# One 512-column operand for the two parts of x in the recurrent passes

## The chip, the cores and the metric

The kernel runs on one core of one Trainium2 chip. Times are device microseconds (us) of that core. The comparison is between the median of several runs of the kernel before and of the kernel after; where the text works from a profile it says so, since that is one execution. The engines are TensorE (PE in the profile; PEld is its weight loading), VectorE (DVE), ScalarE (ACT), GpSimd (POOL) and SyncE (SP), which issues the DMAs.

## The reference, cut to what matters

Two model blocks follow each other, 256 tokens wide 2048 features, in float32. The change lies in the first block alone, in its recurrent branch:

```
xn = rms_norm(x, norm_pre_w)
z = xn @ w_in                       # u_lru: 2048 columns, g_lru: 2048 columns, then q, k, v, gates
u = centred_depthwise_conv(u_lru, conv_w, conv_b)          # 4 taps over the tokens
gate_r = sigmoid(block-wise u @ w_r + b_r); gate_i = sigmoid(block-wise u @ w_i + b_i)
log_a = -8 * gate_r * softplus(-lam);  a = exp(log_a)
b = sqrt(-expm1(2 * log_a)) * (gate_i * u)
h = scan(a, b) forwards + scan(a', b') backwards           # over the 256 tokens
y_a = h * silu(g_lru)
```

The rest of block one (keys and values, attention, merging, output) and two layers of block two come after it and are not touched.

## The kernel before

Every matrix product is made of three float32r products, since one alone is not exact enough: with x = x_hi + x_lo and w = w_hi + w_lo it sums w_hi·x_hi, w_hi·x_lo and w_lo·x_hi. ScalarE rounds each weight slot to w_hi (L273), VectorE subtracts to get w_lo (L281), and TensorE may use the slot when VectorE has counted it in the semaphore `split`. A slot holds 2048 weights per partition. Five slots form a ring; SyncE loads a slot when TensorE has finished with the slot five before it (`used`).

Slots 0 to 31 are the eight recurrent passes, four slots each. In pass i TensorE makes two tiles of u_lru (slots 4i and 4i+1, PSUM banks z0 and z1) and two of g_lru (slots 4i+2 and 4i+3, banks z2 and z3), each of 128 features by 256 tokens. A slot is 16 steps kk of three matmuls of 256 columns (`features`, L308). After them come sixteen matmul instructions for the gates of the recurrence (L1113), which read the convolved u. Slots 32 to 35 make the keys and 36 to 39 the values, with matmuls of 512 columns (`tokens`, L320); after slot 37 the keys are turned (L1146).

The other engines follow with a loop of their own, written out by hand. Its round i does the convolution of pass i and the gates and the scan of pass i-1. ScalarE: sigmoid of g_lru out of PSUM (`gate_inputs`, L560), eight sigmoids of the recurrence's gates (`gates`), rounding of slot 4i+3, four tanh, rounding of slot 4i+4, copy of u_lru out of PSUM (`input_copy`, L598), four exp, one sqrt (L590), rounding of slots 4i+5 and 4i+6, rounding of y (L602). VectorE: product of g_lru with its sigmoid (`open_gates`, L840), residual of slot 4i+3, residual of slot 4i+4, two convolutions (`convolve`, L829 and L833, four instructions each), the recurrence (L846, L850, four scans), residual of slot 4i+5, the output y (L860, L863), residual of slot 4i+6, the residual of y (L867). All engines run their queue strictly in the written order. In round 2 VectorE also prepares the angles of the rotary embedding (L889, L891 ahead of slot 13's residual; L356 to L363 between y and slot 14's residual), and before round 1 it has a chain of small steps for the softplus.

TensorE waits, before slot 4i+b (b = 0, 1), for `ucopied`, which frees bank zb; before slot 4i+2+b for `zcopied`, which frees bank z(2+b); and before the gates of pass i for `conv`, the eight steps of both convolutions.

Of the kernel before, what the change touches and what calls it, by code (L numbers as in the profile page):

```python
# [10 lines left out]
F32R = mybir.dt.float32r  # L11
I32 = mybir.dt.int32
ACT = mybir.ActivationFunctionType
ALU = mybir.AluOpType
AX_X = mybir.AxisListType.X

P = 128
D = 2048
T = 256
KT = D // P  # L20
# [12 lines left out]
LRU_PASSES = KT // 2  # L33
# [214 lines left out]
class Ring:  # L248
# [50 lines left out]
    def features(self, pe, n, out, x_hi, x_lo, each=None, whole=True):  # L299
# [9 lines left out]
        ins.then_inc(self.s.used, 1)  # L309

    def tokens(self, pe, n, quarter, outs, x_hi, x_lo):

        w_hi, w_lo = (w[:, self.place(n)].rearrange("p (k f) -> p k f", k=4) for w in (self.k.w_hi, self.k.w_lo))
        self.await_slot(pe, n)
        for kk in range(4):
            row = 4 * quarter + kk
            for m in range(2):
                t = slice(P * m, P * m + P)
                for j, (x, w) in enumerate(((x_hi, w_hi), (x_hi, w_lo), (x_lo, w_hi))):
                    ins = pe.matmul(outs[m], x[:, row, t], w[:, kk], start=row == 0 and j == 0, stop=row == KT - 1 and j == 2)  # L320
        ins.then_inc(self.s.used, 1)
# [26 lines left out]
def reduce_angles(link, dve, angle, turns, rest, looked):  # L348
# [4 lines left out]
    for n, quarter in enumerate((0.0, 0.25)):  # L353
# [5 lines left out]
        for m, part in enumerate(turn_parts):  # L359
# [5 lines left out]

B1_SEMS = ("loaded0 loaded1 loaded2 loaded3 loaded4 rounded split used "
           "p1_in ident_in consts_in x0 x1 x2 x3 eps squared averaged rooted first0 first1 first2 first_rounded first_split second_rounded second_split scaled ascaled turned xrounded xsplit "
# [8 lines left out]
def first_parts(k, t, s):  # L376
# [68 lines left out]
    def tile(n):  # L445
        return z[n][:, 0:T]
# [67 lines left out]
    def scalar(act):  # L514
# [40 lines left out]
        def gate_inputs(i):  # L555
            act.wait_ge(s.used, 4 * i + 4)
            if i:
                act.wait_ge(s.zcopied, 2 * i)
            for b in range(2):
                act.activation(gsig[:, b], tile(2 + b), ACT.Sigmoid).then_inc(s.gsig, 1)  # L560

# [30 lines left out]
        def input_copy(i, b):  # L592
            act.wait_ge(s.used, 4 * i + b + 1)
            if i:
                act.wait_ge(s.conv, 8 * (i - 1) + 4 * b + 4)
            else:
                act.wait_ge(s.cleared, 1)
            act.activation(padded[:, b, 2:2 + T], tile(b), ACT.Copy).then_inc(s.ucopied, 1)  # L598

# [173 lines left out]
    def vector(dve):  # L773
# [47 lines left out]
        ring.residual(dve, 2)  # L821

        def convolve(i, b):
            dve.wait_ge(s.ucopied, 2 * i + b + 1)
            u = u_all[:, 2 * i + b:2 * i + b + 1]
            for tap in range(4):
# [8 lines left out]
                ins.then_inc(s.conv, 1)  # L835

        def open_gates(i):
            dve.wait_ge(s.gsig, 2 * i + 2)
            for b in range(2):
                dve.tensor_tensor(g_all[:, b], tile(2 + b), gsig[:, b], ALU.mult).then_inc(s.zcopied, 1)  # L840

# [16 lines left out]
        def outputs_lru(i):  # L858
            dve.wait_ge(s.dsteps, 8 * i + 6)
            dve.tensor_tensor(gate_r[:, :, 0], gate_r[:, :, 0], gate_r[:, :, 1], ALU.add).then_inc(s.dsteps, 1)  # L860
            dve.wait_ge(s.zcopied, 2 * i + 2)
            dve.wait_ge(s.dsteps, 8 * i + 7)
            dve.tensor_tensor(y[:], gate_r[:, :, 0], g_all[:], ALU.mult).then_inc(s.dsteps, 1)  # L863
# [6 lines left out]
        for i in range(LRU_PASSES + 1):  # L870
            n = 4 * i
            if i:
                open_gates(i - 1)
            ring.residual(dve, n + 3)
            if i == 0:
# [3 lines left out]
            ring.residual(dve, n + 4)  # L879
            if i < LRU_PASSES:  # L880
                convolve(i, 0)
                convolve(i, 1)
            if i:
# [196 lines left out]
    def tensor(pe):  # L1080
# [42 lines left out]
        for i in range(LRU_PASSES):  # L1123
            for b in range(2):
                if i:
                    pe.wait_ge(s.ucopied, 2 * (i - 1) + b + 1)
                    ring.features(pe, 4 * i + b, tile(b), k.xn_hi, k.xn_lo)
                else:
                    ring.features(pe, b, tile(b), k.xn_hi, k.xn_lo, (first_rows, second_rows)[b], False)
            for b in range(2):  # L1130
                if i:
                    pe.wait_ge(s.zcopied, 2 * (i - 1) + b + 1)
                ring.features(pe, 4 * i + 2 + b, tile(2 + b), k.xn_hi, k.xn_lo)
            gates(i)
# [14 lines left out]

        pe.wait_ge(s.zcopied, 2 * LRU_PASSES)  # L1150
        for w in range(4):
# [154 lines left out]

FIRST_COUNTS = {
    "rounded": 155, "split": 155, "used": 152, "p1_in": 16, "ident_in": 16,
    "consts_in": 32, "x0": 16, "x1": 16, "x2": 16, "x3": 16, "eps": 1, "squared": 4, "averaged": 1, "rooted": 2,
    "first0": 16, "first1": 16, "first2": 16, "first_rounded": 3, "first_split": 3, "second_rounded": 3,  # L1310
    "second_split": 3, "scaled": 6, "ascaled": 2, "turned": 16, "xrounded": 16, "xsplit": 16, "weights0": 64,
    "weights1": 64, "gated": 16, "cleared": 1, "chain": 26, "exped": 1, "ucopied": 16, "conv": 64, "gsig": 16,
    "zcopied": 16, "gates": 8, "taken": 64, "decay": 72, "dsteps": 64, "rounded_y": 8, "ydone": 8, "counted": 1,
    "rotary_in": 16, "rchain": 19, "rlooked": 3, "mask_in": 16, "sink_in": 16, "sinkready": 2, "kcopied": 2,
# [1661 lines left out]
def build(nc, t):  # L2976

    with ExitStack() as stack:
# [20 lines left out]
        k.middle = goto(k.xn_at)  # L2999
        k.xn_hi, k.xn_lo = (put(n, [P, KT, T], F32R) for n in ("xn_hi", "xn_lo"))  # L3000
        goto(k.xn_at)
# [114 lines left out]
```

## Time and profile before

| | us |
|---|---|
| median of 3 runs | 1927.61 |
| lowest and highest | 1927.23 and 1928.36 |
| the profiled execution, its time | 1927.07 |
| its span in the profile | 1925.3 |
| TensorE busy, in the span | 1895.8 (98%) |
| VectorE busy | 1265.1 (66%) |
| ScalarE busy | 1104.7 (57%) |

The recurrent passes take the first 232 us of the span. A matmul's duration in the profile is longer than the distance to the next one, since matmuls are pipelined: the throughput is read from the distance between starts, or from the chain, where a piece of n matmuls stands with its length. "Idle before" a group is the time its engine stood still just ahead of it, with the instruction that ended the wait.

### The profile page before, as it was taken

The page shows a single profiled execution, that of the slowest core. Times are in us where ns is not written, and L with a number is a line of the kernel's source. Part 1 is how long each engine was busy: PE and PEld are TensorE (multiplying, and loading weights), DVE is VectorE, ACT ScalarE, POOL GpSimd, SP SyncE. Part 2 cuts the span into 40 slices and gives each one's busy share as a digit, 9 for nine tenths or more (in the row PEclk, how much of TensorE's full clock was granted, in tenths as well). Part 3 has the DMA queues.
Part 4 walks back from the last instruction along what each step waited for, and adds up shares of the span by engine and source line. Part 5 has one row for each costly group of instructions (what it writes and reads, how often), then busy time and mean ns, then how long its engine had stood idle before and what let it go on. Part 6 is the DMA issues. An engine that isn't in the chain of part 4 may idle for free.

```text
span 1925.3 us, 32036 instructions
## 1 busy us (share of the span) xinstructions
PE 1895.8 (98%) x13736; PEld 1710.5 (89%) x13736; DVE 1265.1 (66%) x1769; ACT 1104.7 (57%) x1510; POOL 70.6 (4%) x66
## 2 busy tenths in 40 slices
PE   7999999999999999999899999999999999999998
PEld 7999989999888888888799999998889999999887
DVE  7778765555544444655689888754648988876453
ACT  6777755454533333434646688836554667893441
POOL 0111100000000000000000000100000000010000
PEclk9999999999999999999999999999999999999999
DMA  6545454444455555565554444322666444432263
GB/s 250 194 176 181 164 188 173 153 154 153 166 189 193 195 197 199 177 260 191 190 212 168 165 148 150 130 74 89 233 220 226 170 159 156 151 125 97 67 227 122
DMA packets 52269, 328.94 MB, mean 171 GB/s; under 512 B 7968, under 2 KB 9888, under 8 KB 14368
## 3 DMA queue, kind: packets, MB, share of 16 engines
q1 hardware_dynamic: 52128, 326.90, 47.2%
q8 instruction: 108, 1.77, 0.4%
q14 instruction: 33, 0.27, 0.0%
HBM read 320.59 MB, written 6.29 MB: 170 GB/s over the span
## 4 chain that ended last, share of the span: by engine, by line
PE 96%; ACT 2%; DVE 1%; issue 0%; DMA 0%; SPq 0%; ACTq 0%; DVEq 0%
PE z L308 43%; PE z L320 38%; PE aux L1113 1%; PE aux L2717 1%; PE z L344 1%; PE z L332 1%; PE aux L1161 1%; PE aux L2619 1%; PE aux L1178 1%; PE aux L2722 1%; PE aux L2581 1%; PE z L2606 1%; ACT w_hi L273 0%; PE aux L2801 0%; DMA x_first<-in_x_dram 0%
## 5 line engine op out<-in xcount | busy, mean ns | idle before, releaser
L281 DVE TENSOR_TENSOR w_lo<-w_raw,w_hi 128x2048 fp32r<-128x2048 f32 x274 | 631.7, 2308 | 364.8 <-ACT w_hi L273 364.4
L273 ACT ACTIVATE w_hi<-w_raw 128x2048 fp32r<-128x2048 f32 x286 | 546.6, 1916 | 418.8 <-DMA w_raw<-in_w_dram 418.8
L308 PE MATMUL z<-xn_hi,w_hi 128*128 128x256 f32 x2112 | 619.5, 293 | 0.0
L308 PE MATMUL z<-xn_lo,w_hi 128*128 128x256 f32 x2112 | 597.5, 283 | 0.0
L308 PE MATMUL z<-xn_hi,w_lo 128*128 128x256 f32 x2112 | 597.5, 283 | 0.0
L308 PEld LDWEIGHTS z<-xn_hi,w_hi 128*128 128x128 f32 x2112 | 404.7, 192 | 15.8 <-issue 12.5
L308 PEld LDWEIGHTS z<-xn_lo,w_hi 128*128 128x128 f32 x2112 | 405.2, 192 | 5.0 <-issue 4.3
L308 PEld LDWEIGHTS z<-xn_hi,w_lo 128*128 128x128 f32 x2112 | 404.8, 192 | 0.0
L320 PE MATMUL z<-w_hi,xn_hi 128*128 128x512 f32 x568 | 223.0, 393 | 0.0
L320 PE MATMUL z<-w_hi,xn_lo 128*128 128x512 f32 x568 | 221.1, 389 | 0.0
L320 PE MATMUL z<-w_lo,xn_hi 128*128 128x512 f32 x568 | 221.0, 389 | 0.0
L320 PE MATMUL z<-w_hi,y_hi 128*128 128x512 f32 x368 | 143.6, 390 | 0.0
L320 PE MATMUL z<-w_hi,y_lo 128*128 128x512 f32 x368 | 143.3, 389 | 0.0
L320 PE MATMUL z<-w_lo,y_hi 128*128 128x512 f32 x368 | 143.2, 389 | 0.0
L320 PEld LDWEIGHTS z<-w_hi,xn_lo 128*128 128x128 f32 x568 | 106.6, 188 | 22.3
L320 PEld LDWEIGHTS z<-w_lo,xn_hi 128*128 128x128 f32 x568 | 106.7, 188 | 21.8
L320 PEld LDWEIGHTS z<-w_hi,xn_hi 128*128 128x128 f32 x568 | 106.7, 188 | 21.5
L2041 DVE SCALAR_TENSOR_TENSOR acc<-padded_b,params,acc 128x256 f32<-128x256 f32 x240 | 98.5, 479 | 0.0
L320 PEld LDWEIGHTS z<-w_hi,y_lo 128*128 128x128 f32 x368 | 69.1, 188 | 14.5
L320 PEld LDWEIGHTS z<-w_lo,y_hi 128*128 128x128 f32 x368 | 69.1, 188 | 14.1
L320 PEld LDWEIGHTS z<-w_hi,y_hi 128*128 128x128 f32 x368 | 69.1, 188 | 14.0
L2195 DVE SCALAR_TENSOR_TENSOR conv<-padded,params,conv 128x256 f32<-128x256 f32 x108 | 58.2, 539 | 31.4 <-ACT conv L1768 28.8
(426 smaller groups left out, 2487.6 us busy)
## 6 DMA issues: line engine op xcount, KB each, us to landing
w_raw<-in_w_dram SPq DMA_DIRECT2D x287, 1024.0 KB, 4.8
gate_w<-in_lru_w_dram SPq DMA_DIRECT2D x8, 512.0 KB, 3.5
x_t<-state_dram SPq DMA_DIRECT2D x2, 2048.0 KB, 9.9
x_first<-in_x_dram SPq DMA_DIRECT2D x4, 512.0 KB, 6.5
x_t<-in_x_dram SPq DMA_DIRECT2D x1, 2048.0 KB, 11.3
state_dram<-x_t SPq DMA_DIRECT2D x2, 1024.0 KB, 5.2
pw<-in_pw_dram SPq DMA_DIRECT2D x2, 1024.0 KB, 6.7
state_dram<-x_t SPq DMA_DIRECT2D x8, 256.0 KB, 6.0
```

Of the source, the lines that this page charges most:

```text
L273: act.activation(self.k.w_hi[:, self.place(n)], self.k.w_raw[:, self.place(n)], ACT.Copy).then_inc(self.s.rounded, 1)
L281: dve.tensor_tensor(self.k.w_lo[:, at], self.k.w_raw[:, at], self.k.w_hi[:, at].bitcast(F32), ALU.subtract)\
L308: ins = pe.matmul(out, w[:, kk], x[:, kk], start=kk == 0 and j == 0, stop=kk == KT - 1 and j == 2)
L320: ins = pe.matmul(outs[m], x[:, row, t], w[:, kk], start=row == 0 and j == 0, stop=row == KT - 1 and j == 2)
L332: ins = pe.matmul(outs[m], x[:, row, t], w[:, kk], start=False, stop=row == KT - 1 and j == 2)
L344: ins = pe.matmul(outs[m], x[:, row, t], w[:, kk, 0:V_COLS], start=row == 0 and j == 0, stop=False)
L1113: ins = pe.matmul(aux[2 * b + d][:, g * T:g * T + T], gate_w[i % 2][:, b, 2 * d + g], u_all[:, 2 * i + b], start=True, stop=True)
L1161: ins = pe.matmul(aux[2 * p + h][:, b * T:b * T + T], q_turned[:, 2 * p + h, P * b:P * b + P], keys[:, c], start=True, stop=True)
L1178: ins = pe.matmul(aux[2 * p][:, h * T:h * T + T], values[:, kb, P * c:P * c + P], S[p][:, h].rearrange("p b t -> p (b t)")[:, kb * T:kb * ...
L2041: dve.scalar_tensor_tensor(out=acc[:, b], in0=padded_b[:, b, n:n + T], scalar=col(w), in1=acc[:, b], op0=ALU.mult, op1=ALU.add).then_inc(s ...
L2195: dve.scalar_tensor_tensor(out=conv[:, i], in0=padded[:, i, tap:tap + T], scalar=col(w), in1=conv[:, i], op0=ALU.mult, op1=ALU.add).then_i ...
L2581: ins = pe.matmul(aux[2 * p + h][:, there], q_rot[here, c, p, P * b:P * b + P], keys[here, kv_of(u, h), 0:P * b + P], start=True, stop=True)
```

## The change

- TensorE: in the 32 slots of the recurrent passes a new helper `halves` takes the place of `features`. The high part and the residual of x now lie in one tensor `xn`, so that one matmul of 512 columns multiplies w_hi with both, into the two halves of a whole PSUM bank; a matmul of 256 columns adds w_lo·x_hi to the first half. A step kk is two matmuls instead of three.
- The two halves of each bank have to be added. For u_lru, ScalarE copies the first half as before (it now counts `uhalf`) and VectorE adds the second half in place (`sum_input`, one instruction ahead of each convolution), which then counts `ucopied`. For g_lru, VectorE sums both halves with a reduction over two (`sum_gates`, two instructions at the start of the round) and counts `zcopied`; ScalarE waits for both and takes the sigmoid out of the sum in SBUF; the product (`open_gates`) moves behind the residual of slot 4i+3 and reads SBUF.

```diff
+    def halves(self, pe, n, bank, x, each=None, whole=True):
+        w_hi, w_lo = (w[:, self.place(n)].rearrange("p (k f) -> p k f", k=KT) for w in (self.k.w_hi, self.k.w_lo))
+        if whole:
+            self.await_slot(pe, n)
+        for kk in range(KT):
+            if each is not None:
+                each(kk)
+            pe.matmul(bank[:, 0:2 * T].rearrange("p (b t) -> p b t", b=2), w_hi[:, kk], x[:, :, kk], start=kk == 0, stop=False)
+            ins = pe.matmul(bank[:, 0:T], w_lo[:, kk], x[:, 0, kk], start=False, stop=kk == KT - 1)
+        ins.then_inc(self.s.used, 1)
...
         def gate_inputs(i):
-            act.wait_ge(s.used, 4 * i + 4)
-            if i:
-                act.wait_ge(s.zcopied, 2 * i)
+            act.wait_ge(s.zcopied, 4 * i + 2)
             for b in range(2):
-                act.activation(gsig[:, b], tile(2 + b), ACT.Sigmoid).then_inc(s.gsig, 1)
+                act.activation(gsig[:, b], g_all[:, b], ACT.Sigmoid).then_inc(s.gsig, 1)
...
-            act.activation(padded[:, b, 2:2 + T], tile(b), ACT.Copy).then_inc(s.ucopied, 1)
+            act.activation(padded[:, b, 2:2 + T], tile(b), ACT.Copy).then_inc(s.uhalf, 1)
...
+        def sum_input(i, b):
+            dve.wait_ge(s.uhalf, 2 * i + b + 1)
+            there = padded[:, b, 2:2 + T]
+            dve.tensor_tensor(there, there, z[b][:, T:2 * T], ALU.add).then_inc(s.ucopied, 1)
...
+        def sum_gates(i):
+            dve.wait_ge(s.used, 4 * i + 4)
+            if i:
+                dve.wait_ge(s.dsteps, 8 * i)
+            for b in range(2):
+                dve.tensor_reduce(g_all[:, b], z[2 + b][:, 0:2 * T].rearrange("p (h t) -> p t h", h=2), AX_X, ALU.add).then_inc(s.zcopied, 1)
...
         def open_gates(i):
             dve.wait_ge(s.gsig, 2 * i + 2)
             for b in range(2):
-                dve.tensor_tensor(g_all[:, b], tile(2 + b), gsig[:, b], ALU.mult).then_inc(s.zcopied, 1)
+                dve.wait_ge(s.zcopied, 4 * i + b + 1)
+                dve.tensor_tensor(g_all[:, b], g_all[:, b], gsig[:, b], ALU.mult).then_inc(s.zcopied, 1)
...
             if i:
+                sum_gates(i - 1)
+            ring.residual(dve, n + 3)
+            if i:
                 open_gates(i - 1)
-            ring.residual(dve, n + 3)
...
             if i < LRU_PASSES:
+                sum_input(i, 0)
                 convolve(i, 0)
+                sum_input(i, 1)
                 convolve(i, 1)
...
-        k.xn_hi, k.xn_lo = (put(n, [P, KT, T], F32R) for n in ("xn_hi", "xn_lo"))
+        k.xn = put("xn", [P, 2, KT, T], F32R)
+        k.xn_hi, k.xn_lo = (k.xn[:, i] for i in range(2))
```

The order on VectorE from the end of round 2 into round 3, before (brackets name the semaphores that a row waits for):

```order
L867 TENSOR_TENSOR y_lo<-y,y_hi 128x512 [waits all_rounded_y]
L840 TENSOR_TENSOR g_all<-z,gsig 128x256 [waits all_gsig]
L840 TENSOR_TENSOR g_all<-z,gsig 128x256
L281 TENSOR_TENSOR w_lo<-w_raw,w_hi 128x2048 [waits all_rounded] x2
L829 TENSOR_SCALAR u_all<-padded,params 128x256 [waits all_ucopied]
L833 SCALAR_TENSOR_TENSOR u_all<-padded,params,u_all 128x256 [waits all_conv] x3
L829 TENSOR_SCALAR u_all<-padded,params 128x256 [waits all_ucopied]
L833 SCALAR_TENSOR_TENSOR u_all<-padded,params,u_all 128x256 [waits all_conv] x3
L846 SCALAR_TENSOR_TENSOR tau<-decay,tau 128x1024 [waits all_decay]
```

And at the same place of the changed kernel:

```order
L890 TENSOR_TENSOR y_lo<-y,y_hi 128x512 [waits all_rounded_y]
L857 TENSOR_REDUCE g_all<-z 128x256 [waits all_dsteps,all_used]
L857 TENSOR_REDUCE g_all<-z 128x256
L281 TENSOR_TENSOR w_lo<-w_raw,w_hi 128x2048 [waits all_rounded]
L863 TENSOR_TENSOR g_all<-g_all,gsig 128x256 [waits all_zcopied,all_gsig]
L863 TENSOR_TENSOR g_all<-g_all,gsig 128x256 [waits all_zcopied]
L281 TENSOR_TENSOR w_lo<-w_raw,w_hi 128x2048 [waits all_rounded]
L836 TENSOR_TENSOR padded<-padded,z 128x256 [waits all_uhalf]
L844 TENSOR_SCALAR u_all<-padded,params 128x256 [waits all_ucopied]
L848 SCALAR_TENSOR_TENSOR u_all<-padded,params,u_all 128x256 [waits all_conv] x3
L836 TENSOR_TENSOR padded<-padded,z 128x256 [waits all_uhalf]
L844 TENSOR_SCALAR u_all<-padded,params 128x256 [waits all_ucopied]
```

Two reductions now stand where the two products stood, the products stand between the two residuals, and one more instruction stands ahead of each convolution.

ScalarE from the rounding of y to the gates, before:

```order
L602 ACTIVATE y_hi<-y 128x512 [waits all_dsteps]
L560 ACT_TABLE_LOAD [waits all_zcopied]
L560 ACTIVATE gsig<-z 128x256 [waits all_used]
L560 ACTIVATE gsig<-z 128x256
L568 ACTIVATE gate_r<-aux,params 128x256 [waits all_gates,all_dsteps]
```

And in the changed kernel:

```order
L612 ACTIVATE y_hi<-y 128x512 [waits all_dsteps]
L570 ACT_TABLE_LOAD
L570 ACTIVATE gsig<-g_all 128x256 [waits all_zcopied]
L570 ACTIVATE gsig<-g_all 128x256
L578 ACTIVATE gate_r<-aux,params 128x256 [waits all_gates,all_dsteps]
```

The sigmoid's wait is now on VectorE's sums of the same round; the table load ahead of it waits for nothing.

## Rows read from the trace of the kernel before

**Rows 1.** Part 1 of the page, busy time and share of the span

```profile
PE 1895.8 (98%) x13736; PEld 1710.5 (89%) x13736; DVE 1265.1 (66%) x1769; ACT 1104.7 (57%) x1510; POOL 70.6 (4%) x66
```

**Rows 2.** The chain that ended last: start us, length us, what; pass 7 onwards

```profile
205.13 23.03 PE z L308 x192
228.16 3.46 PE aux L1113 x16
231.62 32.69 PE z L320 x144
264.31 0.87 PE aux L1146 x8
```

**Rows 3.** Timeline of VectorE, 128 to 154 us: start us, us, instruction [idle before <-releaser]

```profile
128.22 0.69 DVE L863 TENSOR_TENSOR y<-gate_r,g_all 128x512 f32<-128x512 f32 x1
128.83 2.29 DVE L281 TENSOR_TENSOR w_lo<-w_raw,w_hi 128x2048 fp32r<-128x2048 f32 x1
131.03 0.68 DVE L867 TENSOR_TENSOR y_lo<-y,y_hi 128x512 fp32r<-128x512 f32 x1
131.63 0.75 DVE L840 TENSOR_TENSOR g_all<-z,gsig 128x256 f32<-128x256 f32 x2
136.31 2.95 DVE L281 TENSOR_TENSOR w_lo<-w_raw,w_hi 128x2048 fp32r<-128x2048 f32 x1 [3.92 <-ACT w_hi L273]
139.69 2.29 DVE L281 TENSOR_TENSOR w_lo<-w_raw,w_hi 128x2048 fp32r<-128x2048 f32 x1 [0.43 <-ACT w_hi L273]
141.90 0.41 DVE L829 TENSOR_SCALAR u_all<-padded,params 128x256 f32<-128x256 f32 x1
...
145.68 1.22 DVE L846 SCALAR_TENSOR_TENSOR tau<-decay,tau 128x1024 f32<-128x1024 f32 x1
...
150.55 2.26 DVE L281 TENSOR_TENSOR w_lo<-w_raw,w_hi 128x2048 fp32r<-128x2048 f32 x1
...
153.52 0.69 DVE L863 TENSOR_TENSOR y<-gate_r,g_all 128x512 f32<-128x512 f32 x1
```

**Rows 4.** Timeline of ScalarE in the same round

```profile
128.94 0.63 ACT L602 ACTIVATE y_hi<-y 128x512 fp32r<-128x512 f32 x1 [5.04 <-DVE y L863]
129.59 1.28 ACT L560 ACT_TABLE_LOAD   x1
130.89 0.66 ACT L560 ACTIVATE gsig<-z 128x256 f32<-128x256 f32 x2
...
144.54 1.06 ACT L590 ACTIVATE tau<-tau 128x1024 f32<-128x1024 f32 x1
```

**Rows 5.** Timelines of both engines: the start of round 1, and round 2

```profile
46.25 0.47 ACT L568 ACTIVATE gate_r<-aux,params 128x256 f32<-128x256 f32 x1 [2.80 <-PE aux L1113]
...
48.71 0.75 DVE L840 TENSOR_TENSOR g_all<-z,gsig 128x256 f32<-128x256 f32 x2
...
90.06 1.23 DVE L846 SCALAR_TENSOR_TENSOR tau<-decay,tau 128x1024 f32<-128x1024 f32 x1 [1.09 <-ACT tau L590]
...
98.58 0.69 DVE L863 TENSOR_TENSOR y<-gate_r,g_all 128x512 f32<-128x512 f32 x1
...
103.50 2.29 DVE L281 TENSOR_TENSOR w_lo<-w_raw,w_hi 128x2048 fp32r<-128x2048 f32 x1
```

**Rows 6.** Instructions by line and shape: count | busy us, mean ns | idle before

```profile
L2155 DVE TENSOR_REDUCE small<-S 128x2 f32<-128x512 f32 x12 | 8.1, 676 | 0.0
L840 DVE TENSOR_TENSOR g_all<-z,gsig 128x256 f32<-128x256 f32 x16 | 6.0, 416 | 0.0
```

**Rows 7.** Timelines of both engines in round 8, the last

```profile
233.00 0.66 ACT L560 ACTIVATE gsig<-z 128x256 f32<-128x256 f32 x2
...
247.20 1.22 DVE L846 SCALAR_TENSOR_TENSOR tau<-decay,tau 128x1024 f32<-128x1024 f32 x1 [3.10 <-ACT tau L590]
...
255.05 0.69 DVE L863 TENSOR_TENSOR y<-gate_r,g_all 128x512 f32<-128x512 f32 x1
...
259.85 0.29 DVE L920 TENSOR_TENSOR q_tok<-rope_a,rope_b 128x128 f32<-128x128 f32 x1
```

More of the change, by code:

```diff
@@ L363, in reduce_angles @@
         link(lambda: dve.tensor_scalar(rest, rest, -3.1415925, None, ALU.max))
-B1_SEMS = ("loaded0 loaded1 loaded2 loaded3 loaded4 rounded split used "
+B1_SEMS = ("uhalf loaded0 loaded1 loaded2 loaded3 loaded4 rounded split used "
            "p1_in ident_in consts_in x0 x1 x2 x3 eps squared averaged rooted first0 first1 first2 first_rounded first_split second_rounded second_split scaled ascaled turned xrounded xsplit "
@@ L860, in outputs_lru @@
             dve.tensor_tensor(gate_r[:, :, 0], gate_r[:, :, 0], gate_r[:, :, 1], ALU.add).then_inc(s.dsteps, 1)
-            dve.wait_ge(s.zcopied, 2 * i + 2)
+            dve.wait_ge(s.zcopied, 4 * i + 4)
             dve.wait_ge(s.dsteps, 8 * i + 7)
@@ L1126, in tensor @@
                     pe.wait_ge(s.ucopied, 2 * (i - 1) + b + 1)
-                    ring.features(pe, 4 * i + b, tile(b), k.xn_hi, k.xn_lo)
+                    ring.halves(pe, 4 * i + b, z[b], k.xn)
                 else:
-                    ring.features(pe, b, tile(b), k.xn_hi, k.xn_lo, (first_rows, second_rows)[b], False)
+                    ring.halves(pe, b, z[b], k.xn, (first_rows, second_rows)[b], False)
             for b in range(2):
                 if i:
-                    pe.wait_ge(s.zcopied, 2 * (i - 1) + b + 1)
-                ring.features(pe, 4 * i + 2 + b, tile(2 + b), k.xn_hi, k.xn_lo)
+                    pe.wait_ge(s.zcopied, 4 * (i - 1) + b + 1)
+                ring.halves(pe, 4 * i + 2 + b, z[2 + b], k.xn)
             gates(i)
@@ L1148, in turn_heads @@
                     ins.then_inc(out_sem, 1)
-        pe.wait_ge(s.zcopied, 2 * LRU_PASSES)
+        pe.wait_ge(s.zcopied, 4 * LRU_PASSES)
         for w in range(4):
@@ L1307 @@
 FIRST_COUNTS = {
+    "uhalf": 16,
     "rounded": 155, "split": 155, "used": 152, "p1_in": 16, "ident_in": 16,
@@ L1312 @@
     "weights1": 64, "gated": 16, "cleared": 1, "chain": 26, "exped": 1, "ucopied": 16, "conv": 64, "gsig": 16,
-    "zcopied": 16, "gates": 8, "taken": 64, "decay": 72, "dsteps": 64, "rounded_y": 8, "ydone": 8, "counted": 1,
+    "zcopied": 32, "gates": 8, "taken": 64, "decay": 72, "dsteps": 64, "rounded_y": 8, "ydone": 8, "counted": 1,
     "rotary_in": 16, "rchain": 19, "rlooked": 3, "mask_in": 16, "sink_in": 16, "sinkready": 2, "kcopied": 2,
```

## The prediction

> **What bounds the kernel now.** I read the page first: TensorE is busy for 98% of the span [rows 1], so a wait of TensorE that is added anywhere lengthens the run, and nothing later takes it back. The chain that ended last says the same of the recurrent passes: 192 matmuls of 256 columns in 23.03 us without a gap, 3.46 us for the gates, and the next pass [rows 2]. A pass costs TensorE 26.49 us. The 256-column matmuls stand 23.03/192 = 0.1199 us apart, the 512-column ones of the keys 32.69/144 = 0.2270 us [rows 2]: one wide matmul is 0.0129 us cheaper than two narrow ones.
>
> Then I read the timelines of VectorE and ScalarE side by side, since the change gives them work. Neither ever waits for TensorE in the middle passes; they wait for each other. ScalarE stands still 5.04 us for VectorE's y, VectorE 3.92 and 0.43 us for ScalarE's w_hi [rows 3, 4]. From one y to the next are 153.52 - 128.22 = 25.30 us [rows 3]. So this is a closed loop of two engines that runs by its own length, 25.30 us, 1.2 us less than a pass of TensorE. That is its whole margin, and the idle time shown inside it is no reserve: it lies on a path that passes from one engine to the other.
>
> The loop has three pieces. From y's start to the sigmoid of g (gsig): 130.89 - 128.22 = 2.67 us, made of y, the rounding of y and a table load of 1.28 us [rows 3, 4]. From gsig to tau: 145.68 - 130.89 = 14.79 us; both engines arrive together there (ScalarE's sqrt starts at 144.54 and ends at 145.60) [rows 3, 4]. From tau to y: 153.52 - 145.68 = 7.84 us [rows 3]. Sum 25.30.
>
> **The change, TensorE's part.** Of 3 matmuls in a step kk two remain. If a wide one with a split operand costs what the keys' wide ones do, a slot saves 16 x 0.0129 = 0.206 us, a pass 0.82 and the 32 slots 6.6 us. The bound on the other side is nothing saved (the two separate stretches of x cost as two matmuls). TensorE alone would need 26.49 - 0.82 = 25.67 us a pass.
>
> The trace puts the fixed part of a matmul at 0.1199 - 0.1067 = 0.013 us, if the columns stream at 2.4 GHz [rows 2]. The Trainium skill, page "TensorE: Matmul & The Clock Gate", section "Back-to-back issue gap", gives N/2.4 ns plus 2.5 ns for a warm gap; by it the same edit would save 512 x 2.5 ns = 1.3 us. The rows of this trace do not agree with it, and the sum goes by the rows.
>
> **The change, y to gsig.** Before, ScalarE only needed its own table load. Now gsig waits for VectorE's two sums, and these stand in VectorE's queue behind the residual of slot 4i+6 and that of y: they begin where the products began, 131.63 - 128.22 = 3.41 us after y [rows 3]. A reduction over 512 elements took 0.676 us [rows 6]; the second begins about 0.07 before the first ends, so the two take 1.29, and ScalarE starts 0.03-0.04 later. That is 4.74 us instead of 2.67: **+2.07**. The table load no longer has a wait and is hidden in it. The price of a reduction over pairs that lie 256 apart in PSUM is not in the trace: its bounds are 0.42 us (the 256-element product out of PSUM, if it were paid by outputs [rows 6]) and 1.22 us (half the rate, near twice the row). I take 0.68, the nearest row.
>
> **gsig to tau.** The products now stand between the residuals: 0.416 us each, about 0.34 apart [rows 6], they start at 139.18 and push the second residual from 139.69 to 139.87 (+0.18) [rows 3]. Each convolution has an addition ahead of it, which the convolution waits for: 0.42 and the hand-over, 0.45 each, **+0.90** (bounds 0.36 and 0.5). The two convolutions themselves stay at 145.68 - 141.90 = 3.78 us. Together 14.79 + 1.08 = 15.87 us. ScalarE's path alone stays at 14.7. Behind them wait tau, the scans, y and two residuals. Tau to y is unchanged, 7.84. The reads of SBUF in place of PSUM on ScalarE I cost at nothing; they may be 0.1 us a pass.
>
> **The new period** is 4.74 + 15.87 + 7.84 = 28.45 us, above TensorE's 25.67 and above today's 26.49. The loop becomes the bound, and TensorE stops ahead of the gates of each pass for `conv`, and a little ahead of slot 4i+3 for `split`.
>
> **The sum.** I follow gsig, round by round. Round 1: before, gates start at 46.25, which is gsig at 45.71; VectorE was in the softplus chain until 48.71 at no cost [rows 5]. Now the sums are queued behind that chain, which ends 0.90 later (two additions in round 0), so gsig is free at 48.71 + 0.90 + 1.33 = 50.94. Round 2: 50.94 + 28.45 = 79.39. Round 3: tau at 79.39 + 15.87 = 95.26; y after 98.58 - 90.06 = 8.52 (the angle's steps) [rows 5], 103.78; the residual of slot 14 is 103.50 - 98.58 = 4.92 behind y instead of 0.61 [rows 5, 3], so the sums start 7.72 behind y and gsig is at 103.78 + 9.05 = 112.83 (105.59 before, by the same pieces). Rounds 4 to 8 at 28.45 each: round 7 at 226.6, round 8 at 255.1.
>
> The convolutions of pass 7 end 15.92 us behind gsig, at 242.5; the gates take 3.46, and the keys start at 246.0 instead of 231.62 [rows 2]: **+14.4**. In the keys' slots (5.45 us each) the last round is still late. The residual of slot 35 ends 8.40 us behind gsig, at 263.5, where TensorE arrives at 262.3: +1.1. In round 8 gsig to tau is 247.20 - 233.00 = 14.20 and tau to y 7.85 [rows 7]; slot 37's residual ends 7.14 behind tau, at 276.4, TensorE arrives at 274.4: +2.1. The keys' rotation ends 5.05 behind y, at 282.15, 0.3 after TensorE [rows 7]. Total 14.4 + 1.1 + 2.1 + 0.3 = **17.8 us**. On the profiled execution, 1927.07 us, that is **1944.9**; that execution lies 0.5 below the median of the runs, which I leave in the range.
>
> TensorE's own saving does not enter: with nothing saved per matmul the same walk ends at the same 246.0, since VectorE decides from pass 3 on.
>
> **The rivals.**
> - Dear sums: a reduction over far pairs runs at half rate, 1.22 us. Each round grows by 1.07, the period is 29.5, and the total is +26.3: 1953.4. For it: no row has such a pattern. Against: all reductions of the trace go by elements read, 676 ns for 512 [rows 6].
> - Cheap sums and additions (0.42 and 0.36): period 27.7, +12.2: 1939.3.
> - The added work hides (the other side): VectorE idles 3.92 + 0.43 us a round [rows 3], and if the sums and additions fit there, TensorE keeps its gain of 6.6 us: 1920.5. This decides if the period stays under 25.67, 2.8 us less than I count. Against it: the 3.92 lie after the sums, and wait for ScalarE, which itself waits for the sums; the additions stand where VectorE has no gap.
> - The change does not do what it says, the wide matmul costs two narrow ones: no different, 1944.9 as well.
>
> **How the numbers follow.** Forecast with its small variants 0.73, dear sums 0.10, cheap ones 0.08, hidden work 0.06, something near no change (half of the loop's growth eaten by a margin I do not see) 0.03. A measurement of this kernel can tell about 0.2% from no change, 3.9 us. Faster 0.06, same 0.03, slower 0.91. The range leaves out the two last cases and what lies beyond the dear sums: 1937 to 1955.
>
> **What would show it.** In the profile after: no single piece of some 18 us but TensorE idle ahead of the gates (about 2 us a pass, released by VectorE's convolution) and ahead of slots 4i+3 (0.8), with the most in pass 3 (slots 14 and 15, about 2.3 and 3.5); y to y 28.4 us; ScalarE's gsig waiting for the reduction, some 2 us a round; reductions at 0.68; wide and narrow matmul together 0.347 us apart. If y to y is near 25.5, or TensorE shows no wait in the passes, my reading of the loop is wrong. If only the reductions differ from 0.68, two of them times eight rounds give the correction. It would also be wrong if idle times of 2 us lowered TensorE's clock.

## The result, and the profile after

| | before | after |
|---|---|---|
| median of 5 runs, us | 1927.36 | 1945.44 |
| lowest and highest | 1926.5 and 1928.36 | 1944.04 and 1946.93 |
| profiled execution: time, span | 1927.07, 1925.3 | 1945.44, 1943.7 |
| TensorE busy, VectorE busy (profile) | 1895.8, 1265.1 | 1896.7, 1279.8 |

The changed kernel is slower: ratio 1.0095, 95% interval 1.0084 to 1.0105, which is 18.1 us. By the profiled executions it is 18.4.

The page of after, its line of busy times, answers to [rows 1]:

```profile
PE 1896.7 (98%) x13224; PEld 1683.7 (87%) x13224; DVE 1279.8 (66%) x1801; ACT 1105.0 (57%) x1510; POOL 70.6 (4%) x66
```

Nothing on this line tells of 18 us: each share is what it was. The loss is all there when the keys are turned, at 282.58 us in the timeline of TensorE, where the timeline of before has them at 264.15: 18.4 us.

```profile
282.58 1.03 PE L1173 MATMUL aux<-ident,q_tok 128*128 128x128 f32 x8
```

The waits of after in 0 to 300 us (engine, line and what it waited for: us in total, times, longest) name both ends of the matter:

```profile
DVE w_lo L281 <- ACT w_hi L273: 52.4, 12, 5.5
ACT y_hi L612 <- DVE y L886: 41.5, 7, 6.1
ACT gsig L570 <- DVE g_all L857: 26.1, 8, 11.7
...
PE aux L1140 <- DVE u_all L848: 9.8, 6, 1.7
...
PE z L319 <- DVE w_lo L281: 3.6, 5, 1.7
PE z L332 <- DVE w_lo L281: 2.7, 2, 1.8
PE z L319 <- DVE g_all L857: 1.8, 1, 1.8
```

ScalarE's gsig now waits for VectorE's sum (L857) in all eight rounds, and TensorE, which never waited in the middle passes, waits for the convolution ahead of the gates in six of the eight passes (9.8 us), for residuals ahead of slots of the passes (3.6) and of the keys (2.7), and once for a sum (1.8): 17.9 us in all.

VectorE's timeline of after, one round from y to y (start us, us, engine, line, operation, count, idle before it and what ended it), answers to [rows 3]:

```profile
135.38 0.69 DVE L886 TENSOR_TENSOR y<-gate_r,g_all 128x512 f32<-128x512 f32 x1
135.99 2.28 DVE L281 TENSOR_TENSOR w_lo<-w_raw,w_hi 128x2048 fp32r<-128x2048 f32 x1
138.20 0.69 DVE L890 TENSOR_TENSOR y_lo<-y,y_hi 128x512 fp32r<-128x512 f32 x1
138.80 1.28 DVE L857 TENSOR_REDUCE g_all<-z 128x256 f32<-128x512 f32 x2
145.60 2.94 DVE L281 TENSOR_TENSOR w_lo<-w_raw,w_hi 128x2048 fp32r<-128x2048 f32 x1 [5.52 <-ACT w_hi L273]
148.46 0.75 DVE L863 TENSOR_TENSOR g_all<-g_all,gsig 128x256 f32<-128x256 f32 x2
149.13 2.28 DVE L281 TENSOR_TENSOR w_lo<-w_raw,w_hi 128x2048 fp32r<-128x2048 f32 x1
151.33 0.41 DVE L836 TENSOR_TENSOR padded<-padded,z 128x256 f32<-128x256 f32 x1
...
153.67 0.41 DVE L836 TENSOR_TENSOR padded<-padded,z 128x256 f32<-128x256 f32 x1
...
156.01 1.22 DVE L869 SCALAR_TENSOR_TENSOR tau<-decay,tau 128x1024 f32<-128x1024 f32 x1
...
163.85 0.69 DVE L886 TENSOR_TENSOR y<-gate_r,g_all 128x512 f32<-128x512 f32 x1
```

From y to y are 163.85 - 135.38 = 28.47 us, where they were 25.30. VectorE's longest gap has grown too, to 5.52 us, while the round became longer: the idle time was no reserve. ScalarE in the same round, against [rows 4]:

```profile
136.11 0.63 ACT L612 ACTIVATE y_hi<-y 128x512 fp32r<-128x512 f32 x1 [6.09 <-DVE y L886]
136.76 1.28 ACT L570 ACT_TABLE_LOAD   x1
140.11 0.72 ACT L570 ACTIVATE gsig<-g_all 128x256 f32<-128x256 f32 x2 [2.06 <-DVE g_all L857]
```

The table is loaded by 138.04, then ScalarE stands for 2.06 us until the sums are there.

### The profile page after: what moved, and what is told of

Read it like the earlier page. It is cut to its first block, busy times and chain, and to the rows that moved or that the text cites. A ratio compares the mean times of both kernels' runs of the same rounds, so it can differ in the third digit from the quotient of the medians.

```text
span 1943.7 us, 31052 instructions
## 1 busy us (share of the span) xinstructions
PE 1896.7 (98%) x13224; PEld 1683.7 (87%) x13224; DVE 1279.8 (66%) x1801; ACT 1105.0 (57%) x1510; POOL 70.6 (4%) x66
## 4 chain that ended last, share of the span: by engine, by line
PE 83%; DVE 9%; ACT 5%; issue 2%; DMA 0%; SPq 0%; DVEq 0%; ACTq 0%
PE z L332 36%; PE z L308 34%; DVE w_lo L281 3%; PE aux L2745 1%; ACT w_hi L273 1%; PE z L356 1%; DVE u_all L848 1%; PE z L344 1%; PE aux L1188 1%; PE aux L2647 1%; PE aux L1205 1%; ACT gate_i L580 1%; ACT gate_r L578 1%; PE aux L2750 1%; PE aux L2609 1%
## 5 line engine op out<-in xcount | busy, mean ns | idle before, releaser
L308 PE MATMUL z<-xn,w_hi 128*128 128x256 f32 x3200 | 599.7, 289 | 0.0
L308 PEld LDWEIGHTS z<-xn,w_hi 128*128 128x128 f32 x3200 | 499.3, 191 | 20.2 <-issue 17.1
L308 PE MATMUL z<-xn,w_lo 128*128 128x256 f32 x1600 | 452.2, 283 | 0.0
L332 PE MATMUL z<-w_hi,xn 128*128 128x512 f32 x1136 | 356.8, 392 | 2.7 <-DVE w_lo L281 2.7
L308 PEld LDWEIGHTS z<-xn,w_lo 128*128 128x128 f32 x1600 | 306.1, 191 | 0.0
L332 PEld LDWEIGHTS z<-w_hi,xn 128*128 128x128 f32 x1136 | 214.2, 189 | 47.5 <-DVE w_lo L281 3.5
L332 PE MATMUL z<-w_lo,xn 128*128 128x512 f32 x568 | 221.8, 390 | 0.0
L319 PE MATMUL z<-xn,w_hi 128*128 128x512 f32 x512 | 185.2, 405 | 5.4 <-DVE w_lo L281 3.6
L320 PE MATMUL z<-xn,w_lo 128*128 128x256 f32 x512 | 143.9, 281 | 0.0
L332 PEld LDWEIGHTS z<-w_lo,xn 128*128 128x128 f32 x568 | 107.0, 188 | 21.8
L319 PEld LDWEIGHTS z<-xn,w_hi 128*128 128x128 f32 x512 | 97.1, 190 | 29.8 <-issue 5.1
L320 PEld LDWEIGHTS z<-xn,w_lo 128*128 128x128 f32 x512 | 97.6, 191 | 0.2
```

The costliest lines, as they stand in the source:

```text
L308: ins = pe.matmul(out, w[:, kk], x[:, kk], start=kk == 0 and j == 0, stop=kk == KT - 1 and j == 2)
L319: pe.matmul(bank[:, 0:2 * T].rearrange("p (b t) -> p b t", b=2), w_hi[:, kk], x[:, :, kk], start=kk == 0, stop=False)
L320: ins = pe.matmul(bank[:, 0:T], w_lo[:, kk], x[:, 0, kk], start=False, stop=kk == KT - 1)
```

## Experiments

Each was compared with the kernel before on the same chip. The first four take the change apart.

**The matmuls kept narrow.** In 15 of 16 steps of a slot the wide matmul is two narrow ones again; all sums and additions stay:

```diff
-            pe.matmul(bank[:, 0:2 * T].rearrange("p (b t) -> p b t", b=2), w_hi[:, kk], x[:, :, kk], start=kk == 0, stop=False)
+            if kk == 0:
+                pe.matmul(bank[:, 0:2 * T].rearrange("p (b t) -> p b t", b=2), w_hi[:, kk], x[:, :, kk], start=True, stop=False)
+            else:
+                pe.matmul(bank[:, 0:T], w_hi[:, kk], x[:, 0, kk], start=False, stop=False)
+                pe.matmul(bank[:, T:2 * T], w_hi[:, kk], x[:, 1, kk], start=False, stop=False)
```

> The changed kernel with the wide matmuls taken back: in 15 of the 16 steps of a slot three matmuls of 256 columns, the one with the residual of x into the second half of the bank; all sums and additions on VectorE stay. Theory (the closed loop of VectorE and ScalarE sets the pace, TensorE's form is hidden): y to y 28.45 us as in the changed kernel, TensorE idle 1.7 to 1.8 us ahead of the gates of passes 3 to 7, about 1944.7 us (up to 1946.6 if TensorE's clock falls ahead of the last keys slot as it did in the changed kernel). Rival (the wide matmul or its strided operand is what costs): back near 1927 us.

Measured 1946.43 (4 runs; ratio 1.0100, 1.0085 to 1.0115). y to y is 28.46 again. TensorE, with 0.8 us more work in a pass, stops for 1.50 us ahead of the gates instead of 1.69 (gates of pass 4), and no longer ahead of slot 4i+3, where it stood up to 0.6 us. What the wide matmul saves does not reach the end of the run while the sums are there.

**The wide matmuls without the sums.** The second halves of the banks are computed and not read, so w_hi·x_lo is missing in the 32 slots; VectorE and ScalarE do what they did before. Of VectorE's part, against the changed kernel:

```diff
-                sum_gates(i - 1)
...
-                sum_input(i, 0)
-                sum_input(i, 1)
...
-                dve.tensor_tensor(g_all[:, b], g_all[:, b], gsig[:, b], ALU.mult).then_inc(s.zcopied, 1)
+                dve.tensor_tensor(g_all[:, b], tile(2 + b), gsig[:, b], ALU.mult).then_inc(s.zcopied, 1)
```

> The changed kernel with the wide matmuls kept and the element-wise work of before: no sums, no additions, the second half of each bank is never read, so the product of w_hi with the residual of x is missing from u and g in the recurrent passes. Theory: y to y 25.3 us, below TensorE's 25.7 a pass, no stop of TensorE, and its gain stands free: 32 slots at 0.206 us are 6.6 us, with up to 1.1 us more from the first slot, where TensorE ran ahead in the changed kernel: 1919.3 to 1920.8 us. Rival by the Trainium skill's gap of 2.5 ns a matmul: 1.3 us, about 1926 us. Rival (wide matmuls cost): 1927 or more.

Measured 1920.68 (6 runs; ratio 0.997, 0.9958 to 0.9982). From VectorE's timeline of this kernel:

```profile
150.72 0.69 DVE L887 TENSOR_TENSOR y<-gate_r,g_all 128x512 f32<-128x512 f32 x1
...
176.01 0.69 DVE L887 TENSOR_TENSOR y<-gate_r,g_all 128x512 f32<-128x512 f32 x1
```

y to y is 25.29, TensorE never stops in the passes, and the gates start 25.65 us apart in five of seven passes, as 26.49 - 0.82 says. So the wide matmuls are worth 6.4 us, and the sums cost them and 18 more. Not all of the 6.4 is the price of a matmul: in the trace the first gates come 1.5 us earlier than before (41.08 and 42.59), where a pass saves 0.8, and two passes last 26.06 us. In these two TensorE does not wait either: a step of a wide and a narrow matmul takes 0.353 us in them, from the first slot to the last, and 0.347 in the other five. Why is open.

**The two sums apart.** Wide matmuls and additions in the u slots alone (`features` stays in the g slots), and the other way round. TensorE's line of the first:

```diff
-                ring.halves(pe, 4 * i + 2 + b, z[2 + b], k.xn)
+                ring.features(pe, 4 * i + 2 + b, tile(2 + b), k.xn_hi, k.xn_lo)
```

> Only the u half of the change: wide matmuls and the two additions for slots 4i and 4i+1; slots 4i+2 and 4i+3, the sigmoid and the product of g as before. Theory: the additions lengthen y to y by 0.90 us to 26.2, still a little more than TensorE's pass of 26.08; the loop's head start is used up only by pass 7. TensorE gains 3.3 us and the start's 1 us and loses about 1 us in the keys' slots: 1923.9 us. Rival (the additions are what makes the changed kernel slow): above 1935 us.

> Only the g half of the change: wide matmuls, the two reductions ahead of the sigmoid and the moved products for slots 4i+2 and 4i+3; slots 4i and 4i+1 as before. Theory: y to gsig +2.07, gsig to tau +0.18, so y to y 27.55 us, TensorE idle about 1.1 us ahead of the gates of passes 3 to 7 and 0.4 ahead of slots 4i+3, 3.5 in pass 3: 1937.5 us, up to 1939.4 if its clock falls in the keys' slots. Rival (the reductions' own 1.29 us per round is the price, not the place where they stand): y to y 26.6 us and 1930 us or less.

The u slots alone: 1925.65 (10 runs; 0.9993, 0.9984 to 1.0003), y to y 26.20. The g slots alone: 1938.24 (4 runs; 1.0057, 1.0042 to 1.0072), y to y 27.55. One y and the next in the first trace, then in the second:

```profile
154.21 0.69 DVE L887 TENSOR_TENSOR y<-gate_r,g_all 128x512 f32<-128x512 f32 x1
...
180.42 0.69 DVE L887 TENSOR_TENSOR y<-gate_r,g_all 128x512 f32<-128x512 f32 x1
```

```profile
132.88 0.69 DVE L886 TENSOR_TENSOR y<-gate_r,g_all 128x512 f32<-128x512 f32 x1
...
160.43 0.69 DVE L886 TENSOR_TENSOR y<-gate_r,g_all 128x512 f32<-128x512 f32 x1
```

Over 25.30 that is +0.90 and +2.25, and together 3.15 of the 3.17 measured. The additions cost what I gave them, and so do the sums with the shifted residual (2.07 + 0.18). The two sums themselves last only 1.29 us a round; they cost 2.07, since they stand behind two residuals and ScalarE's table load no longer fills the time. The u slots alone came 1.8 us above what was expected. Of that, 1.0 is the start (the first gates at 42.17, 0.4 us earlier than before, where I had given 1.0 and the pass's own 0.4), 0.4 the passes, since the loop's 26.20 lies a little above the 26.08 that TensorE needs there, and 0.2 the keys' slots.

**Repairing the order.** If the loss is the length of the loop and not the work, the sums can be made in the place where VectorE's neighbour waits for nothing: right behind y of the round before, ahead of a residual and the residual of y, while ScalarE rounds y and loads its table.

```diff
             if i:
-                sum_gates(i - 1)
+                open_gates(i - 1)
             ring.residual(dve, n + 3)
-            if i:
-                open_gates(i - 1)
...
                 outputs_lru(i - 1)
+            if 0 < i < LRU_PASSES:
+                sum_gates(i)
...
             else:
+                sum_gates(0)
```

> The changed kernel with the same instructions in another order on VectorE: the two sums of g right behind y of the round before (in round 0 ahead of the softplus chain), the products ahead of the residual of slot 4i+3 again, where VectorE idles. Theory (the place of the sums is the price, not their 1.29 us): the sums are ready 1.93 us behind y, before ScalarE needs them at 2.67, so y to y is 25.30 + 0.90 = 26.2 us; TensorE idle 1.8 us ahead of the gates of pass 3, then 0.5 in each pass, and 1.2 in the keys' slots: 1924.7 us. Rival (VectorE's work counts wherever it stands): y to y 27.5, about 1937 us.

Measured 1927.86 (10 runs; 1.0004, 0.9994 to 1.0013): with the same instructions in another order, 0.8 of the 18 us are left. Its VectorE:

```profile
156.08 0.69 DVE L886 TENSOR_TENSOR y<-gate_r,g_all 128x512 f32<-128x512 f32 x1
156.88 1.29 DVE L857 TENSOR_REDUCE g_all<-z 128x256 f32<-128x512 f32 x2
```

and ScalarE's gsig starts 2.67 us behind y as before the change (158.75 - 156.08). It still missed what was expected by 3.2 us. One of them is in the sum: the stops that I had named (1.8 in pass 3, 0.5 in each of the four passes behind it, 1.2 in the keys' slots) make 1925.7 on top of the 1920.68 of the kernel without sums, and not 1924.7. More than named was lost in pass 3, where the angle's steps lengthen VectorE's round (28.78 us, 3.1 over 25.65, with these two stops):

```profile
114.78 0.47 PE L319 MATMUL z<-xn,w_hi 128*128 128x512 f32 x1 [0.87 <-DVE w_lo L281]
...
122.12 1.13 PE L1141 MATMUL aux<-u_all,gate_w 128*128 128x256 f32 x4 [1.55 <-DVE u_all L848]
```

From there on TensorE follows the loop's 26.27 us a pass, 0.6 above its own 25.65, and the keys' slots cost 1.3.

**Shortening the loop as well.** Beside that, ScalarE rounds slot 4i+3 ahead of the sigmoids, VectorE takes its residual ahead of the products, and on both engines the copies and convolutions come ahead of slot 4i+4. ScalarE's part:

```diff
+            ring.round(act, n + 3)
             if i:
                 gate_inputs(i - 1)
                 gates(i - 1)
-            ring.round(act, n + 3)
-            if i:
                 tanhs(i - 1)
-            ring.round(act, n + 4)
             if i < LRU_PASSES:
                 input_copy(i, 0)
                 input_copy(i, 1)
+            ring.round(act, n + 4)
```

> As the kernel with the early sums, and further: ScalarE rounds slot 4i+3 ahead of the sigmoids and copies u ahead of rounding slot 4i+4; VectorE takes the residual of slot 4i+3 in its idle time, and the additions and convolutions ahead of the residual of slot 4i+4. Theory: the additions then lie beside ScalarE's path, y to y is bound by that path or by TensorE's pass, 25.3 to 25.7 us, no stop of TensorE but some 1.5 us in the keys' slots: 1921.3 us. Rival (VectorE's extra 2.2 us a round cannot be hidden): 1924 or more.

> The kernel before, narrow matmuls and no sums, with the new order of roundings, copies, convolutions and residuals alone. Theory: TensorE bounds the passes with no stop, so the order gives nothing: 1927 us, within 0.1% of the kernel before. Rival (the order, not the wide matmuls, is what the version with all of it gains): 1924 or less.

The whole: 1925.49 (10 runs; 0.9993, 0.9983 to 1.0002), y to y 25.47:

```profile
154.63 0.69 DVE L885 TENSOR_TENSOR y<-gate_r,g_all 128x512 f32<-128x512 f32 x1
...
180.10 0.69 DVE L885 TENSOR_TENSOR y<-gate_r,g_all 128x512 f32<-128x512 f32 x1
```

The new order in the kernel before, without the change: 1927.31 (10 runs; 1.0001, 0.9992 to 1.0011), no difference. The order is worth nothing by itself there, since TensorE is the bound and the loop's length is hidden. The first of the two missed by 4.2 us. Its time lies in the range of its rival, which said that VectorE's added work can't be hidden; the period of 25.47, under TensorE's 25.65, says that in the passes it is, and the trace tells where the time went. Two stops of TensorE, and then stretches of 2 us (sum, busy us of PE, PEld, VectorE, ScalarE and GpSimd, granted clock, DMA share, GB/s) around the second:

```profile
128.60 0.47 PE L319 MATMUL z<-xn,w_hi 128*128 128x512 f32 x1 [0.54 <-DVE w_lo L281]
...
255.32 0.50 PE L332 MATMUL z<-w_hi,xn 128*128 128x512 f32 x1 [1.80 <-DVE w_lo L281]
```

```profile
254.00:256.00 2.00, 0.68 (x3) 0.58 (x4) 1.90 (x3) 0.00 (x0) 0.00 (x0) 1.00 0.62 176
256.00:258.00 2.00, 2.00 (x7) 1.51 (x6) 2.00 (x2) 1.30 (x3) 0.00 (x0) 0.50 0.83 348
258.00:260.00 2.00, 2.00 (x7) 1.60 (x6) 1.97 (x6) 2.00 (x3) 0.00 (x0) 0.64 0.00 0
```

The stop ahead of slot 37 is the last round's, which no later pass covers; behind it TensorE ran at 0.50, 1.2 GHz of its 2.4, for over 3 us. From the gates of pass 7 to the turning of the keys it took 39.86 us, where the kernel without sums took 36.11.

**The last round.** In it, the rounding and the residual of slot 37 go ahead of the recurrence (on top of the last order, and then in the changed kernel alone). VectorE's part:

```diff
+            if i == LRU_PASSES:
+                ring.residual(dve, n + 5)
             if i:
                 scan(i - 1)
...
-            ring.residual(dve, n + 5)
+            if i < LRU_PASSES:
+                ring.residual(dve, n + 5)
```

> As the version with the full new order, and in the last round the rounding and the residual of slot 37 ahead of the recurrence. Theory: the stop of TensorE ahead of slot 37 goes (1.3 us), and with it a possible fall of its clock there: 1919.9 us. Rival (TensorE's own gain is smaller than 0.0129 us a step, or the passes have stops that I do not see): 1921.5 or more.

> The changed kernel with one edit: in round 8 the rounding and the residual of slot 37 stand ahead of the recurrence. It sizes the part of the loss that comes after the last gates. In the trace of the changed kernel TensorE stops 1.79 us ahead of slot 37 (275.42), and then works for 3.4 us at a granted clock of 0.50, so that the keys are turned at 282.58. With slot 37's residual early both should go: TensorE arrives at the turning at 275.42 - 1.79 + 5.45 = 279.1. But the round still ends with the rotation of the keys: tau starts 1.86 later (one more rounding ahead of it on ScalarE), y follows 5.8 behind tau, at 275.9, the rotation ends 5.1 behind y, at 281.0, against 281.16 before. So TensorE should wait for the rotation instead (1.6 us in front of the turning, and some 0.4 in the middle of it, as the order of e8 showed), and slot 38 should start at 281.8 instead of 283.37: 1.5 us are won, 1943.9, and the 1.79 of the stop are not won, since the rotation takes their place. Theory (the clock's fall cost 1.4 us of the 18 because it came where nothing else was waited for): 1943.4 to 1944.4. Rival (the fall was covered by the rotation and cost nothing): 1945.2 to 1945.8. Rival (stop and fall were both on the path and nothing stands behind them): 1945.4 - 3.7 = 1941.8.

With all of it: 1924.59 (10 runs; 0.9987, 0.9978 to 0.9997), 2.4 us or 0.1% below the kernel before; of the versions that compute the whole result it is the only one whose interval leaves out 1, and by little. It missed by 4.7, and lies in the range of its rival, that the passes have stops which I did not see. The stop of slot 37 is gone and another is in its place, for the rotated keys:

```profile
259.92 0.30 PE L1179 MATMUL aux<-ident,q_tok 128*128 128x128 f32 x1 [1.24 <-DVE q_tok L953]
260.63 0.55 PE L1179 MATMUL aux<-ident,q_tok 128*128 128x128 f32 x3 [0.41 <-DVE q_tok L953]
```

These 1.65 us and the 0.65 ahead of slot 17 are 2.3 of the miss. Another 0.8 lie in the expectation itself, which stood that far under the 1920.68 of the kernel without sums, though that one has the whole saving and no stop. Two passes lasted 26.06 us instead of 25.65 without a stop or a lower clock, as two do in the kernel without sums. The rest, 1.6 us, is not located. In the changed kernel alone the edit gave 1945.29 (4 runs, 1944.99 to 1945.80; 1.0093, 1.0078 to 1.0108). That is above what was expected and in the range of the rival by which the fall had cost nothing; but it is also within what the executions of the changed kernel scatter, 1944.04 to 1947.23, so the time decides nothing. The trace speaks against that rival: the rotation ended 5.1 us behind y, TensorE waited 1.14 + 0.41 us for it, and slot 38 began at 282.38. All rounds of that trace run 0.7 us later than those of after, so this answers to 281.7 there, where after had 283.37 with a fall of the clock in slot 37, and 281.97 without one (below). So the 1.79 us ahead of slot 37 are not won by removing that stop, the rotation takes their place, and the fall alone was worth 1.4, by two traces of one kernel.

**The changed kernel once more.**

> The changed kernel, unchanged. Its five executions lay 2.9 us apart (1944.04 to 1946.93), those of the kernel before 1.9. In the one with a trace TensorE stopped some 1.6 to 1.8 us nine times, and after two of these stops its granted clock was 0.50 for about 3.5 us (in 111 to 116 and in 275 to 280); the order that had one such stop at the same place ahead of slot 37 showed the fall in one kernel (e6) and not in another (e4). Theory: whether a stop of this length is followed by a fall is not set by its length, and differs between executions of the same kernel; each fall on the path costs 1.5 to 1.9 us, which makes the spread. Then this trace shows the same stops (within 0.1 us up to the first fall) and falls at other places or in another number, and the executions spread over some 3 us again, around 1945.4, the longer ones at a lower mean clock. Rival: the falls are the same two in each execution, and the spread has another source; then this trace shows them at 112 and at 276 again.

Measured 1946.52 (4 runs, 1944.05 to 1947.23; 1.0101, 1.0084 to 1.0117); its profiled execution took 1944.05. It shows the stops of the trace of after in the same places, within 0.04 us (111.04, 120.18, 127.66 and so on to 275.43); their lengths differ by up to 0.34 us in passes 4 to 7, and by 0.01 ahead of slots 35 and 37. Granted clocks in the two traces, first after, then this one:

```profile
112.00:114.00 2.00, 2.00 (x8) 1.71 (x7) 0.00 (x0) 2.00 (x7) 0.00 (x0) 0.50 0.69 291
...
276.00:278.00 2.00, 2.00 (x6) 1.54 (x6) 1.94 (x2) 1.21 (x3) 0.00 (x0) 0.50 0.89 377
278.00:280.00 2.00, 2.00 (x8) 1.63 (x7) 2.00 (x5) 2.00 (x2) 0.00 (x0) 0.72 0.00 0
```

```profile
112.00:114.00 2.00, 2.00 (x9) 1.71 (x8) 0.00 (x0) 2.00 (x7) 0.00 (x0) 0.50 0.62 262
...
276.00:278.00 2.00, 2.00 (x10) 1.67 (x9) 1.92 (x2) 1.20 (x3) 0.00 (x0) 1.00 0.83 348
278.00:280.00 2.00, 2.00 (x10) 1.65 (x10) 2.00 (x5) 2.00 (x2) 0.00 (x0) 1.00 0.00 0
```

The fall at 112 is in both and the fall at 276 in one. Without it the keys are turned at 281.01 instead of 282.58, and the execution is 1.39 us shorter.

## Why the prediction came out right

The forecast was 1944.9, the median 1945.44. Step by step:

- **The loop bounds the changed kernel.** Right. Predicted y to y 28.45, measured 28.47; its pieces are 4.73 from y to gsig (4.74 predicted), 15.90 from gsig to tau (15.87), 7.84 from tau to y (7.84). A reduction took 0.68 us, so the dear and the cheap sums both fall.
- **TensorE's saving does not enter.** Right: kept narrow, the kernel is no different within the measurement (1.0100 and 1.0095, with overlapping intervals).
- **The wide matmul saves 0.0129 us.** Right: a wide and a narrow one take 0.347 us together in about half of the passes' time in after, though 0.353 in the rest, which I had not foreseen; and without the sums the gain is 6.4 us where 6.6 were worked out; that these are so close is in part luck, since the earlier start and the two long passes of that trace nearly cancel. The passes alone, 25.65 for 26.49, give 0.0131 a step. The rule with 2.5 ns of the Trainium skill, page "TensorE: Matmul & The Clock Gate", section "Back-to-back issue gap", which is given there for a single matmul, would have given 1.3; this run speaks against it for these float32r matmuls.
- **Where TensorE stops.** Right in the places and the releasers, somewhat high in the sizes: 1.6 to 1.7 us ahead of the gates instead of about 2, and 0.3 to 0.6 ahead of slots 4i+3 instead of 0.8. In the trace of after:

```profile
111.07 0.51 PE L319 MATMUL z<-xn,w_hi 128*128 128x512 f32 x1 [1.81 <-DVE g_all L857]
...
120.22 0.47 PE L319 MATMUL z<-xn,w_hi 128*128 128x512 f32 x1 [1.71 <-DVE w_lo L281]
...
148.68 0.47 PE L319 MATMUL z<-xn,w_hi 128*128 128x512 f32 x1 [0.62 <-DVE w_lo L281]
...
156.15 1.13 PE L1140 MATMUL aux<-u_all,gate_w 128*128 128x256 f32 x4 [1.69 <-DVE u_all L848]
...
262.44 0.50 PE L332 MATMUL z<-w_hi,xn 128*128 128x512 f32 x1 [0.86 <-DVE w_lo L281]
...
275.42 0.57 PE L332 MATMUL z<-w_hi,xn 128*128 128x512 f32 x1 [1.79 <-DVE w_lo L281]
```

  In pass 3 they are smaller than I said (1.81 and 1.71, not 2.3 and 3.5). The second is, because TensorE ran slot 14 partly at half clock and so arrived late; in the kernel with narrow matmuls, whose clock stayed up there, it was 3.12. So this fall cost nothing: slot 15 waits for VectorE either way. Slots 35 and 37 have 0.86 and 1.79 where 1.1 and 2.1 were predicted.
- **The sum, 17.8 us.** The keys are turned 18.4 us later (282.58 and 264.15 in the timelines; the chain has 264.31 in [rows 2]). That 17.8 comes so near is in part luck: two terms in it are off and nearly cancel. The walk's start was 1.2 too late: round 1's gsig stood at 49.74, not 50.94, as the first slots ended earlier in that trace (the first gates are at 41.10; 42.59 before, and 40.74 to 42.39 in the other traces, so the start itself moves by over a microsecond). And the granted clock, which I had named only as a thing that could go wrong, without a price or a chance, cost 1.4 to 1.6 in slot 37. Without the fall the forecast would have been about a microsecond too high: the execution with none there has the keys turned at 281.01 and took 1944.05.
- **The hidden-work rival.** It fell, but less far than the 0.06 that I gave it sounds: it asked for a period under 25.67 us, and moving the same instructions, and ScalarE's beside them, brought the period to 25.47. In that order the added work does hide in the passes. What made the change slow is where the sums and additions stood (2.25 and 0.90 us of the period), not that VectorE did them.

What failed were expectations afterwards: that for the u slots (1.8 us too low), those for the three repaired orders (3.2, 4.2 and 4.7) and that for the last round alone (1.4 too low). All five are too low. The first gave the start too much; those for the orders took the stops in pass 3 and in the keys' slots too small or not at all, and priced the clock at nothing; in the last the whole trace ran 0.7 us late.

Open are why some stretches have steps of 0.353 and not 0.347 us at full clock (the passes of 26.06 instead of 25.65 us), 1.6 us of the last order's miss, and what the longer executions of the changed kernel had more. Its nine executions lie at 1944.04 to 1944.20 (three), 1945.44 (one) and 1946.49 to 1947.23 (five); the five have no trace. Their mean granted clocks are 0.995 to 0.997 and those of the first three 0.997 and 0.998, which fits one more fall, but it was not seen.

## What to carry to other kernels

When two engines hand work to each other in a circle, measure the circle's period (from one instruction to the same in the next round) and compare it with the bound's; that difference is the margin, 1.2 us here, and idle time inside the circle is none. An instruction put on the side of the circle that is waited for costs its full time each round or more (here 0.90 us for two additions, and 2.07 for two sums that last 1.29), and the same instruction put where the other engine is busy with something of its own costs little or nothing: here all but 0.8 of 18 us came back by order alone. After such a repair, the rounds that differ from the others (here the third and the last) hold what is left.

## What the runs showed of the hardware

A stop of TensorE of 1.8 us can cost twice. Ahead of slot 37 TensorE stopped 1.78 to 1.80 us in five traces, with no other stop in the 11 us ahead: in three of them (after, the narrow matmuls, the shortened loop) the granted clock then was 0.50 for about 3.5 us, and in two (the g slots alone, the changed kernel once more) it stayed at 1.00. Two of the five are the same kernel, with this stop of 1.79 us at the same time to 0.01 us. Longer stops had no fall behind them: 2.91 us ahead of slot 15 in the g slots alone, 3.12 in the narrow matmuls. So neither the stop's length nor the program decided, and what did is open. The 24 wide matmuls of slot 37 took 282.58 - 275.42 = 7.16 us where the clock was at 0.50 for part of them, and 281.01 - 275.43 = 5.58 where it stayed up. The trace of before, without stops in these passes, has no stretch of 2 us under 0.99 from 20 to 320 us.

A reduction over pairs that lie 256 elements apart in PSUM (L857) cost 0.680 us for 512 elements read, where the maxima over neighbours of [rows 6] cost 0.676, and the 256-element product cost 0.411 us with both inputs in SBUF and 0.416 with one in PSUM.

The steps of a wide and a narrow matmul came at two distances, 0.347 and 0.353 us, at a granted clock of 1.00 for both. In the kernel without sums passes 3 and 6 (92.4 to 118.4 and 169.7 to 195.8 us) have the longer one throughout and the others the shorter; the narrow passes of before last 26.48 to 26.49 us each.
